# A fixed-schedule decoder trunk on one core: the first token half of each output projection runs four K units ahead of the second instead of two

## The reference: what is computed

```
m, v = gmlp_mixer(hn, ...)            # layer 0; layer 1: rglru_mixer; each ends in (... ) @ w_out
x = x + rms_norm(m, g[1])
f = swiglu(rms_norm(x, g[2]), ffn_w_in[li], ffn_w_out[li])     # (silu(g) * u) @ w_out
x = x + rms_norm(f, g[3])
```

## Time and profile before

| | |
|---|---|
| median of 3 runs | 1558.51 us (1558.06 to 1560.34) |
| the profiled execution | 1558.27 us, its span 1556.8 us |
| PE busy | 1516.0 us, 97% of the span |
| DVE / ACT / POOL busy | 978.2 / 685.2 / 295.5 us |
| mean granted TensorE clock | 0.986 of full |

### The profile page before, as it was taken

How to read it: one execution, slowest core, us unless ns; L and a number is a source line. 1 busy time by engine, 2 the same in 40 slices (tenths; PEclk the granted TensorE clock), 3 DMA queues, 4 the chain that set the end, 5 groups by cost and what they waited for, 6 DMA issues and landing times.

```text
span 1556.8 us, 27667 instructions
## 1 busy us (share of the span) xinstructions
PE 1516.0 (97%) x10866; PEld 1489.7 (96%) x10866; DVE 978.2 (63%) x1295; ACT 685.2 (44%) x1120; POOL 295.5 (19%) x260
## 2 busy tenths in 40 slices
PE   7999999999999999999999999997989999999997
PEld 7999999999999899999999998997989999999996
DVE  6454666766343788777753548858588877665434
ACT  5344432224342444555552434383543555554433
POOL 0100033333000311121200014528032121210002
PEclk9999999999999999999999999998999999999998
DMA  7322233232223122333232241221212323233211
GB/s 235 103 81 74 73 102 94 80 97 85 82 82 90 46 65 76 104 86 102 72 132 68 82 122 41 69 61 62 84 39 85 92 81 108 81 95 105 89 38 65
DMA packets 170507, 133.48 MB, mean 86 GB/s; under 512 B 4888, under 2 KB 147504, under 8 KB 170292
## 3 DMA queue, kind: packets, MB, share of 16 engines
q1 hardware_dynamic: 168756, 128.30, 27.6%
q0 software_dynamic: 1664, 3.95, 0.9%
HBM read 128.92 MB, written 3.29 MB: 85 GB/s over the span
## 4 chain that ended last, share of the span: by engine, by line
PE 87%; DVE 6%; POOL 3%; ACT 3%; issue 2%; DMA 0%; SPq 0%; ACTq 0%; POOLq 0%; DVEq 0%
PE ps L550 86%; DVE yb L1693 1%; DVE acc L1449 1%; DVE hl L1480 1%; POOL wide L2106 1%; DVE acc L1459 1%; ACT whi L985 0%; DVE hl L1741 0%; ACT wide L1393 0%; POOL sout L2105 0%; POOL s L2113 0%; DMA wide<-in_x_prompt_dram 0%; PE ps L612 0%; POOL sout L2104 0%; ACT wide L1399 0%
## 5 line engine op out<-in xcount | busy, mean ns | idle before, releaser
L550 PE MATMUL ps<-hh,whi 128*128 128x288 f32 x2624 | 640.3, 300 | 19.4 <-DVE hl L1480 6.6
L550 PE MATMUL ps<-hh,wlo 128*128 128x288 f32 x2624 | 631.2, 296 | 0.0
L550 PE MATMUL ps<-hl,whi 128*128 128x288 f32 x2624 | 630.4, 296 | 0.0
L550 PEld LDWEIGHTS ps<-hh,whi 128*128 128x128 f32 x2624 | 447.8, 190 | 27.4 <-issue 12.5
L550 PEld LDWEIGHTS ps<-hl,whi 128*128 128x128 f32 x2624 | 447.9, 190 | 0.6
L550 PEld LDWEIGHTS ps<-hh,wlo 128*128 128x128 f32 x2624 | 448.3, 190 | 0.0
L1432 DVE TENSOR_TENSOR wlo<-stage,whi 128x1024 fp32r<-128x1024 f32 (+2 forms) x176 | 208.8, 1191 | 249.5 <-ACT whi L985 249.2
L985 ACT ACTIVATE whi<-stage 128x1024 fp32r<-128x1024 f32 (+2 forms) x176 | 173.9, 996 | 393.1 <-PE ps L550 377.5
L550 PE MATMUL ps<-eh,whi 128*128 128x288 f32 x512 | 151.6, 296 | 0.3 <-DVE wlo L1753 0.3
L550 PE MATMUL ps<-el,whi 128*128 128x288 f32 x512 | 151.1, 295 | 0.0
L550 PE MATMUL ps<-eh,wlo 128*128 128x288 f32 x512 | 150.6, 294 | 0.0
(11 more groups left out here) (194 smaller groups left out, 1665.5 us busy)
## 6 DMA issues: line engine op xcount, KB each, us to landing
stage<-in_ffn_w_in_dram SPq DMA_DIRECT2D x88, 512.0 KB, 4.0
stage<-in_ffn_w_out_dram SPq DMA_DIRECT2D x40, 512.0 KB, 3.9
stage<-in_gm_w_in_dram SPq DMA_DIRECT2D x32, 384.0 KB, 3.7
stage<-in_gm_w_in_dram SPq DMA_DIRECT2D x24, 512.0 KB, 3.8
stage<-in_gm_w_out_dram SPq DMA_DIRECT2D x24, 512.0 KB, 3.8
stage<-in_rg_w_in_dram SPq DMA_DIRECT2D x16, 512.0 KB, 4.0
stage<-in_rg_w_out_dram SPq DMA_DIRECT2D x8, 512.0 KB, 3.7
wide<-in_x_prompt_dram SPq DMA_DIRECT2D x2, 1024.0 KB, 7.1
```

What stands on the lines that cost most here:

```text
L550: return pe.matmul(out, w, x, start=start, stop=stop, skip_group_check=more)
```

## The change

In the second group of every output projection the last four units are now the ones that run half by half (three in RO, which has four units), where it was two. The first group keeps two. Around it the hand-written order of ACT and DVE is changed: the splits of the next projection's first three weight units now stand inside the chain of half 0, and more feature tiles of that chain stand ahead of half 1's tiles. No instruction with data is added or removed; SP's list is the same. The diff, cut to its core:

```diff
@@ PE out_phase @@
                 for G in range(2):
                     first = base[name] + G * per
-                    for j in range(per - 2):
+                    apart = range(per - (min(4, per - 1) if G else 2), per)
+                    for j in range(apart[0]):
...
                     for h in range(2):
-                        for j in (per - 2, per - 1):
+                        for j in apart:
...
-                                if (G, h, j) == (1, 1, per - 2):
+                                if (G, h, j) == (1, 1, apart[0]):
                                     if m == 1:
                                         post_sums(p, 0)
@@ ACT out_phase @@
-                    if n > base["GO"] and n + 2 < base["END"]:
+                    if n > base["GO"] and n + 2 < base["END"] and s + 2 < 2 * per:
                         split_hi(n + 2, width_of(n + 2))
...
                                     if NEXT[name]:
-                                        split_hi(n + 3)
+                                        split_hi(n + 1)
                                     post_rb(p, 0)
                                     if NEXT[name]:
                                         high(NEXT[name], 0, 0)
-                                if (G, h, m) == (1, 1, 1) and NEXT[name]:
-                                    high(NEXT[name], 0, 1)
+                                        high(NEXT[name], 0, 1)
+                                        split_hi(n + 2)
+                                        high(NEXT[name], 0, 2)
+                                        high(NEXT[name], 0, 3)
+                                        split_hi(n + 3)
+                                if (G, h, m) == (1, 1, 0) and NEXT[name]:
+                                    high(NEXT[name], 0, 4)
@@ ACT first_tiles @@
-                high(name, 0, 2)
                 act.wait_ge(unit_done, seq(n))
                 y_out(p, 1, 1, 3)
-                high(name, 0, 3)
+                high(name, 0, 5)
+                high(name, 0, 6)
                 post_std(p, 1)
-                high(name, 0, 4)
                 split_hi(n + 3)
-                high(name, 0, 5)
+                high(name, 0, 7)
                 post_rb(p, 1)
-                high(name, 0, 6)
-                high(name, 0, 7)
@@ DVE out_phase @@
-                                    if NEXT[name]:
-                                        normed(p, 0, 1)
-                                        split_lo(n + 3)
-                                        low(NEXT[name], 0, 0)
                 if NEXT[name]:
+                    n = base[name] + 2 * per
+                    normed(p, 0, 1)
+                    split_lo(n)
+                    low(NEXT[name], 0, 0)
                     normed(p, 0, 2)
+                    low(NEXT[name], 0, 1)
+                    split_lo(n + 1)
+                    normed(p, 0, 3)
+                    low(NEXT[name], 0, 2)
+                    normed(p, 0, 4)
+                    low(NEXT[name], 0, 3)
+                    split_lo(n + 2)
+                    normed(p, 0, 5)
@@ DVE first_tiles @@
-                for k in range(1, 4):
-                    normed(p, 0, k + 2)
-                    low(name, 0, k)
-                    post_add(p, 1, 1, k)
+                post_add(p, 1, 1, 0)
+                low(name, 0, 4)
                 normed(p, 0, 6)
-                low(name, 0, 4)
-                post_diag(p, 1)
+                post_add(p, 1, 1, 1)
+                post_add(p, 1, 1, 2)
                 normed(p, 0, 7)
                 low(name, 0, 5)
+                post_add(p, 1, 1, 3)
+                low(name, 0, 6)
+                post_diag(p, 1)
                 split_lo(n + 3)
-                low(name, 0, 6)
                 normed(p, 1, 0)
@@ DVE, the end of the program @@
-                    if h == 0 and k in (1, 2, 3):
-                        post_add(p, 1, 1, k)
-                    if (h, k) == (0, 4):
+                    if h == 0 and k in (5, 6):
+                        post_add(p, 1, 1, 2 * (k - 5))
+                        post_add(p, 1, 1, 2 * (k - 5) + 1)
+                    if (h, k) == (0, 7):
                         post_diag(p, 1)
```

More of the change, by code:

```diff
@@ L1663, in out_phase @@
                     n = base[name] + s
-                    if n + 2 < base["END"]:
+                    if s + 2 < 2 * per:
                         split_lo(n + 2, width_of(n + 2))
-                    if s + 2 < 2 * per:
                         wide_lo(name, s + 2)
@@ L1670, in out_phase @@
                             for m in range(4):
-                                if s // per == 1 and h == 1 and m > 0:
+                                if s // per == 1 and h == 1:
                                     break
```

## The result

The changed kernel took 1546.62 us (median of 4 runs, 1545.70 to 1548.42) against 1558.99 us of the kernel before beside it (4 runs, 1558.06 to 1560.34): ratio 0.9918, 95% interval 0.9903 to 0.9933. It is 12.4 us faster. 1554.1 was forecast, in a range from 1549.0. A second measurement of the same kernel gave 1549.11 us (6 runs, 1545.67 to 1552.89) against 1556.65 us, ratio 0.9946 (0.9930 to 0.9962). The gain is there both times. Its size was smaller the second time, though the two intervals still touch.

What follows compares the result with a forecast made beforehand. PE was taken as the bound (busy 1516.0 of 1556.8 us), with DVE bounding from the start of half 1. GO -1.55, FO0 -1.55 - 1.2, RO +1.55, end -1.4: -4.15 from 1558.27 gives 1554.1 us, range 1549.0 to 1558.8.

Steps and rivals of the forecast that it cites:

- the end: Program's end after FO1: sums 1.1 us earlier, `normed` of half 1 1.1 to 1.7 us earlier; taken as -1.4 us.
- GO's passage: From GO to the next input projection: sums 0.7 us earlier, `normed` of half 1 another 0.85; -1.55 us.
- FO0's passage: From FO0 to the next input projection: -1.55 us as behind GO, and 1.2 us more from a cheaper clock fall.
- RO's passage: Behind RO: chain 3.12 us later for the missing unit, less 1.55 us won; +1.55 us, a loss.
- GO's price: Cost of the clock's fall behind GO, 1.7 us against 3.4 behind the others; taken for FO0 too, 1.2 us won.
- the step named for the 0.85: Tile 6's high and low parts placed ahead of `rb`, so `normed` of half 1 begins 0.85 us earlier at a passage.
- Rival (1): The clock stays full behind GO and FO0: -7.7 us in all, 1550.6 us; chance 0.18.
- Rival (3): Half 1's copies come too late, sums 3.1 us later at each passage: +5.2 us, 1563.4 us; chance 0.08.

Runs made afterwards that it cites:

- the filled kernel: The kernel before with 11 matmuls of 128x128, results unused, added at each of three passages where PE stands waiting; 1555.27 us, ratio 0.9983.
- the experiment on the copies: The changed kernel with ACT's third weight split ahead of high part 3 instead of behind it; 1549.86 us, ratio 0.9952 against the kernel before.

## Why the prediction was wrong, point by point

The direction was right and the size was not: 4.15 us forecast, 12.6 us between the two spans. By the prediction's own terms (FI1 and FO1 are counted up to half 0's last square of FO1, the end from there on, both without the lead):

| term | forecast | measured in the traces |
|---|---|---|
| GO's passage | -1.55 | -3.24 |
| FO0's passage | -2.75 | -4.45 (960.50 - 551.07 against 953.10 - 548.12) |
| RI, RG-LRU and RO up to half 0's last square, without the lead | 0 | -1.81 |
| RO's passage | +1.55 | -0.68 (-3.12 + 41.89 - 39.45) |
| FI1 and FO1 | 0 | +0.12 |
| the end | -1.4 | -2.79 |
| later start of the execution | 0 | +0.29 |

**The step that failed is the clock**: "so I expect the clock to fall again", with GO's price taken for FO0 and RO's left as it was. Its premise failed too. PE's standing time from the projection's end to the sums was put at 3.6 us, "about as long as now" (3.1); behind GO and FO0 it measured 2.1 us (0.53 + 0.52 + 1.06). The wait before tile 0 was put at 1.3 us and is 0.53, in part because GO's last multiplication starts at 520.55 in the trace of before, where the prediction has its end at 520.39:

```profile
520.55 0.29 PE L550 MATMUL ps<-hh,wlo 128*128 128x288 f32 x1
```

Laid end to end, the steps gave the sums to 0.1 us behind GO. From the sums to the last K tile the forecast had 21.95 us behind GO and FO0 and 23.25 behind RO. Measured were 20.27, 20.28 and 20.25 us (548.12 - 527.85, 953.10 - 932.82, 1148.94 - 1128.69). That is 1.7, 1.7 and 3.0 us, 6.4 in all. The absent falls are 4.9 of it: before, 1.2 behind GO and 2.4 and 2.5 behind the others, less the 1.2 that the forecast already counted for FO0. The other 1.5 are the order. Where no fall came, the old order took 22.10 us from the sums of half 1 to the next norm's, and the new one takes 20.8: 1.3 us at each passage, where 0.85 was forecast. And the step named for the 0.85 wins nothing without a fall, as the run with one high part ahead of `rb` shows, so this term came near by luck. Rival (1) named this for GO and FO0, and its 3.25 and 4.55 us fit the measured 3.24 and 4.45. That agreement is partly luck as well: it puts the whole surplus on the clock, and over a quarter of it is the order's. No case priced RO rightly. There the clock did fall for 6.8 us, but mostly while PE stood waiting for ACT, and the distance was 0.8 us longer for it (41.89 against 41.08 in the second trace of the changed kernel). The forecast kept the price of a fall behind the sums although the same text put a 4.4 us stand ahead of them (3.7 measured).

**The end** was the right mechanism at half its size. The sums came 1.0 us sooner, as forecast. `normed` of half 1 starts 4.34 us after the last multiplication instead of 6.25, 1.9 us sooner, and the eight tiles behind it take 1.0 us less to the program's end. Some 0.2 us of this is the clock's: the filled kernel, which keeps the old order and had no fall at its last `rb`, takes 17.54 us from the sums to the end, the kernel before 17.75. That the missing backlog on POOL pays a second time there is read from the traces, not tested.

**RI to RO** changed no instruction ahead of RO's second group. These windows cover the RG-LRU stretch, before and after:

```profile
1063.00:1094.00 31.00, 24.83 (x143) 24.10 (x144) 23.89 (x21) 14.03 (x19) 22.40 (x29) 0.78 0.17 51
```

```profile
1056.00:1087.00 31.00, 26.21 (x158) 25.60 (x159) 23.91 (x21) 14.55 (x21) 22.03 (x29) 0.83 0.18 53
```

0.78 against 0.83 of full over 31 us is 6.8 against 5.1 us lost (the shares are rounded): the 1.7 us here is one fall fewer. It isn't something that the edit does: in the second trace of the changed kernel the same stretch lost 6.8 us again.

**What held.** The lead moves half 0 by 6.24 us (3.12 in RO), and the chain behind it takes most of it back: 4.1 us by the new order against the 36.9 us of the old one without falls. Net of the clock the lead is worth 2.1 us each behind GO and FO0, costs 1.0 us behind RO and brings 2.8 at the end. Without the clock the forecast was -2.95 us and the traces give about -5.6, so the chain itself was undersized too, at the passages by 0.5 us each and at the end by over 1 us. The wait for the low parts is replaced by one for the copies. Rival (3) saw the danger there; the experiment on the copies shows that DVE's steps cover it.

**What stays open** is when the clock falls. Counted over all traces, up to the last K tile of half 1:

| order and lead, and PE's standing time from the projection's end to the sums of half 1 | passages | with a fall |
|---|---|---|
| old order (before, and one high part ahead of `rb`), 3.1 us | 6 | 5 |
| old order with two more splits in the chain, 2.7 to 3.6 us | 3 | 3 |
| old order with PE's waits filled, 0.4 to 0.5 us | 3 | 0 |
| new order, a lead of four, 2.1 us | 9 | 0 |
| the same with the copies early, 2.2 us | 2 | 1 |
| new order, a lead of three or two (RO in the changed kernel among them), 3.3 us and more | 10 | 10 |

So the absent falls behind GO and FO0 are no chance of one trace. PE stands less there than before, and falls became rare; the filled kernel, where only PE's standing was changed, points the same way. But in three of the nine passages the clock fell for 3.4 us just behind the last K tile, in the filled kernel in all three, and nothing here tells why it falls in one run and not in the next. In the two traces of before and after 7.0 of the 12.6 us hang on the clock (1.2 behind GO, 2.4 behind FO0, 1.7 in RG-LRU, 1.7 behind RO). It is the likeliest cause of the two different ratios, which wasn't tested.

## What to carry to other kernels

Giving one half a longer lead buys its chain time, but the lead can push work into that same chain and use the time up. Measure the distance from the chain's first to its last step, once with the lead alone changed and once with the order alone, since both together show neither. Price a fall of the clock by what sets the end where it falls: here one under a wait for another engine cost 0 to 0.8 us, and one under a PE that never waits cost half its length, 1.7 or 3.4 us. The longest new wait in a profile can be harmless; shorten it alone before working on it.

## What the hardware showed that was not expected

In the one execution that was traced, 11 small matmuls in PE's waits kept the clock up through each passage and no further. It fell for 3.4 to 6.8 us behind the next wait, about 20 us on. Two executions of one and the same kernel had the clock at full and at 0.66 over the same 5 us behind FO0.
